# An encoder layer on one core: queries, keys and values of all heads projected in a stage of their own, attention loading finished heads, and GpSimd copying the experts' row numbers

## The reference, cut to what matters

```
q = (rmsnorm(c_q, q_norm_g) @ w_uq).reshape(b, s, N_HEADS, QK_NOPE + QK_ROPE)
kv = (rmsnorm(c_kv, kv_norm_g) @ w_ukv).reshape(b, s, N_HEADS, QK_NOPE + V_DIM)
q = jnp.concatenate([q[..., :QK_NOPE], apply_rope(q[..., QK_NOPE:], cos, sin)], axis=-1)
k = jnp.concatenate([kv[..., :QK_NOPE], jnp.broadcast_to(k_pe, ...)], axis=-1)
...
scores = jnp.einsum('bqhd,bkhd->bhqk', qb, k)
p = jax.nn.softmax(scores, axis=-1)
...
xe = xf[idx]
ye = (silu(xe @ w_gate) * (xe @ w_up)) @ w_down * gates
out = jnp.zeros_like(xf).at[idx].add(ye)
```

## Time and profile before

| | us |
|---|---|
| median of 3 runs | 4414.47 (4413.76 to 4425.7) |
| the profiled execution | 4414.98, span 4413.2 |
| in_proj, without its first loads | about 394 |
| att1, att0 | 1100, 361 |
| experts | 1740 |

### The profile page before, as it was taken

The page is one execution under the profiler, slowest core; times in us unless marked ns, Lnnn a source line. Parts: engine busy times, 40 slices in busy tenths (PEclk is TensorE's granted clock), DMA queues, the critical chain, the costliest instruction groups (busy, mean ns, idle before and its releaser), DMA issues. The chain is left out here.

```text
span 4413.2 us, 56151 instructions
## 1 busy us (share of the span) xinstructions
PE 3867.6 (88%) x19385; PEld 3141.3 (71%) x19385; DVE 2195.6 (50%) x3666; ACT 1947.7 (44%) x3429; POOL 1224.1 (28%) x954
## 2 busy tenths in 40 slices
PE   7799789999999989975999149999999999999992
PEld 1799656766666755653776039999999999999991
DVE  0322167777777756666222764444444444444443
ACT  0444257666667756652322024333343334333432
POOL 0000047767667756652111050000000000000000
PEclk9899889999999989996999559999999999999996
DMA  7221300000000010015443034544444444454436
GB/s 257 99 75 68 99 2 7 4 8 6 8 6 5 6 48 6 13 32 177 153 152 121 2 115 140 155 148 147 143 143 143 151 153 143 145 154 148 143 110 247
DMA packets 296384, 428.21 MB, mean 97 GB/s; under 512 B 43558, under 2 KB 206246, under 8 KB 295050
## 3 DMA queue, kind: packets, MB, share of 16 engines
q1 hardware_dynamic: 269900, 327.41, 22.6%
q0 software_dynamic: 13824, 50.34, 5.1%
q10 hardware_dynamic: 12480, 48.24, 2.8%
HBM read 335.88 MB, written 90.06 MB: 97 GB/s over the span
## 5 line engine op out<-in xcount | busy, mean ns | idle before, releaser
L1114 POOL TENSOR_TENSOR att_pr<-att_e,att_pr 128x512 fp32r<-128x512 f32 x640 | 816.1, 1288 | 399.5 <-ACT att_pr L919 383.6
L982 DVE TENSOR_REDUCE att_mx<-att_m_ps 128x1 f32<-128x512 f32 x640 | 423.0, 680 | 217.6 <-PE att_m_ps L722 214.8
L1954 ACT ACTIVATE moe_wh<-moe_raw 128x1024 fp32r<-128x1024 f32 x384 | 373.9, 1045 | 302.2 <-DMA moe_raw<-w_up 179.5
L913 ACT ACTIVATE att_e<-att_s_ps 128x512 f32<-128x512 f32 x640 | 378.8, 592 | 276.2 <-PE att_s_ps L783 167.6
L1875 POOL DMA_INDIRECT s_x<-moe_ye,moe_to_add x48 | 75.9, 1581 | 1446.0 <-issue 1159.6
L2001 DVE TENSOR_TENSOR moe_wl<-moe_raw,moe_wh 128x1024 fp32r<-128x1024 f32 x384 | 444.5, 1220 | 40.5 <-ACT moe_wh L1954 40.5
L795 PE MATMUL att_o_ps<-att_pr,att_v 128*128 128x512 f32 x1280 | 410.6, 402 | 9.6 <-issue 6.9
L919 ACT ACTIVATE att_pr<-att_e 128x512 fp32r<-128x512 f32 x640 | 402.4, 629 | 16.9 <-issue 1.9
L1911 PE MATMUL moe_a_ps<-moe_xh,moe_wh 128*128 128x384 f32 x1024 | 351.0, 343 | 46.8 <-DVE moe_hf L2029 43.8
L1028 DVE TENSOR_TENSOR att_acc_ps<-att_acc_ps,att_e 128x512 f32<-128x512 f32 x544 | 374.3, 688 | 16.2 <-ACT att_e L913 10.5
L1912 PE MATMUL moe_a_ps<-moe_xl,moe_wh 128*128 128x384 f32 x1024 | 348.7, 341 | 0.0
(11 more groups left out here) (238 smaller groups left out, 7786.0 us busy)
## 6 DMA issues: line engine op xcount, KB each, us to landing
moe_raw<-w_gate SPq DMA_DIRECT2D x64, 1024.0 KB, 5.3
moe_raw<-w_up SPq DMA_DIRECT2D x64, 1024.0 KB, 7.8
moe_raw<-w_down SPq DMA_DIRECT2D x64, 1024.0 KB, 6.7
ada_wa<-w_ada SPq DMA_DIRECT2D x12, 2048.0 KB, 10.0
s_x<-outp_x ACTq DMA_DIRECT2D x24, 512.0 KB, 5.4
s_xn<-outp_xn ACTq DMA_DIRECT2D x24, 512.0 KB, 6.4
fin_x<-s_x SPq DMA_DIRECT2D x12, 1024.0 KB, 12.0
inp_x<-x_sample SPq DMA_DIRECT2D x8, 1024.0 KB, 5.2
```

What stands on the lines that cost most here:

```text
L913: nc.scalar.activation(e[:, s % RING, :], s_ps[s % 2][:, :], ACT.Exp, scale=SCALE).then_inc(exp_done, 1)
L982: nc.vector.tensor_reduce(mx[:, u % CB, u // CB:u // CB + 1], m_ps[u % MB][:, :], AX, ALU.max).then_inc(max_part, 1)
L1114: nc.gpsimd.tensor_tensor(pr[:, s % RING, 1, :], e[:, s % RING, :], pr[:, s % RING, 0, :].bitcast(F32), ALU.subtract).then_inc(lo_done, 1)
L1954: nc.scalar.activation(wh[:, s, part, :], raw[:, s, part, :], ACT.Copy).then_inc(w_hi_done, 1)
```

## The change

`in_proj` stores the latents already split, without the gain: ACT's `latent_high` takes three high parts, DVE three low parts behind the `u_ps` copy, and PE's next turn of latents waits for those (`ct_lo_done`). The rotary key is stored split too, per tile.

A new stage, `latent_proj` (tiles `prj_...`), loads `w_uq` and `w_ukv`, multiplies them by the gain and splits them, and goes over 6 blocks of 512 tokens. Per block PE fills 16 PSUM banks in the order ORDER: four each of keys, queries and values, two of rotary queries (`r`), two of the same with their halves exchanged (`t`). ACT and DVE make high and low parts, and SP stores them to `s_qn`, `s_qr`, `s_kn` and `s_v`.

`attention` no longer projects: SP loads a head's split queries, keys and values into one of HU buffers (2 in att1, 4 in att0) while the head before it is worked on. Its maxima have three PSUM banks (MB = 3) in place of two. In `experts` POOL makes the two copies of row numbers, and DVE waits for `added` only before it writes `ye`.

```diff
@@ in_proj, VectorE, after the copy of u_ps
+                    dve.wait_ge(ct_hi_done, 3 * (n + 1))
+                    hi, lo = (ct[:, n % 2, i, :] for i in range(2))
+                    nc.vector.tensor_tensor(lo[:, 0:BANK], c_ps[0][:, :], hi[:, 0:BANK].bitcast(F32), ALU.subtract)
+                    nc.vector.tensor_tensor(lo[:, BANK:], c_ps[1][:, 0:P], hi[:, BANK:].bitcast(F32), ALU.subtract)
+                    nc.vector.tensor_tensor(krt[:, n % 2, 1, :], c_ps[1][0:ROPE, P:2 * P],
+                                            krt[:, n % 2, 0, :].bitcast(F32), ALU.subtract).then_inc(ct_lo_done, 1)
                     if j == 1 and b + 2 < NB:
                         norm(b + 2)
...
@@ latent_proj, TensorE
+            for b in range(NB):
+                pe.wait_ge(ct_in[b % 2], 16 * (b // 2 + 1))
+                for n, (kind, i) in enumerate(ORDER):
...
+                    ks = KQ if kind in "qrt" else KKV
+                    for k in range(ks):
...
+                        nc.tensor.matmul(dst, a_hi, b_hi, start=(k == 0), stop=False)
+                        nc.tensor.matmul(dst, a_hi, b_lo, start=False, stop=False)
+                        mm = nc.tensor.matmul(dst, a_lo, b_hi, start=False, stop=(k == ks - 1))
+                    mm.then_inc(ready, 1)
...
@@ attention, SyncE
+            def load_qk(n, i):
+                for dst, src in ((q[0:NOPE, i], w["s_qn"]), (q[NOPE:QK, i], w["s_qr"]), (k[0:NOPE, i], w["s_kn"])):
+                    sp.dma_start(dst.bitcast(F32), src[:, bass.ds(n, 1), :, tokens]
+                                 .rearrange("l o r t -> (o r) l t")).then_inc(qk_in[i], 16)
...
@@ attention, TensorE, in body
-                    if kt == KSTEP and project:
...
-                        project_k(x_ps, j, 1 - h)
...
-                    if kt == QPROJ and project:
-                        pe.wait_ge(k_lo_done, hp * NG + NQB + b + 1)
-                        project_q(1 - h, j)
...
@@ experts, GpSimd
+                for s in range(SLOTS):
+                    if not is_first(e):
+                        pool.wait_ge(added[s], e * 16)
+                nc.gpsimd.tensor_copy(to_add[:, :].unsqueeze(1), keep["index"][:, bass.ds(e, 1), :]).then_inc(add_index, 1)
+                pool.wait_ge(ye_done, (e + 1) * DOWNS)
```

More of the change, by code:

```diff
@@ L214, in in_proj @@
         ut = m.sb("ut", [P, 2, UG, T])
-        ct = m.sb("ct", [P, 2, KC * P])
-        krt = m.sb("krt", [ROPE, TOKENS])
-        gain = m.sb("gain", [P, KC])
+        ct = m.sb("ct", [P, 2, 2, KC * P], F32R)
+        krt = m.sb("krt", [ROPE, 2, 2, P], F32R)
         eps = m.sb("eps", [P, 1])
@@ L686, in body @@
+            load_qk(0, 0)
+            for i in range(HU):
+                sp.dma_start(k[NOPE:QK, i].bitcast(F32), w["s_kr"][:, :, tokens]
+                             .rearrange("l r t -> r l t")).then_inc(kpe_in, 16)
+            load_v(0, 0)
+            for i in range(1, HU):
+                load_qk(i, i)
+                load_v(i, i)
+            def body(it, last):
                 for b in range(NG):
                     h, j = b // NQB, b % NQB
-                    if j == 0 and not last:
-                        sp.wait_ge(q_ready, hp * NG + (h + 1) * NQB)
-                        load_weights(hp * 2 + h + 2, h)
@@ L691, in body @@
[L691 to L696 removed]
+                    if j == 0 and from_start(it, h - 1) and not (last and h >= 1):
+                        sp.wait_ge(values_done, it * PER + h * NQB * NT)
+                        load_qk(it * HU + h - 1 + HU, (h - 1) % HU)
+                        load_v(it * HU + h - 1 + HU, (h - 1) % HU)
@@ L697, in _ @@
+                    if from_start(it, b - 1):
+                        store(it, b - 1)
+            over_heads(sp, body)
+            store(ITERS, -1)
             for i in range(2):
-                sp.wait_ge(att_stored[i], 16 * PAIRS * NQB)
+                sp.wait_ge(att_stored[i], 16 * HEADS * NQB // 2)
         @block.tensor
         def _(pe):
-            def project_k(out, j, k0):
-                for k in range(KKV):
-                    mm = nc.tensor.matmul(out[0:NOPE, :], wk[:, k0, k, :], ct_cols(KQ + k, j),
-                                          start=(k == 0), stop=(k == KKV - 1))
-                mm.then_inc(k_ready, 1)
@@ L929, in body @@
+            def body(it, last):
                 for s in range(PER):
                     b, kt, h, j = at(s)
-                    project = not (last and h == 1)
                     if kt == NT - 1 and not (last and b == NG - 1):
-                        act.wait_ge(nmx_turned, hp * NG + b + 2)
+                        act.wait_ge(nmx_turned, it * NG + b + 2)
                         max_row(*after(b))
-                    if from_start(hp, s - 1):
-                        high(hp, s - 1)
-                    exps(hp, s)
@@ L1053, in body, with output @@
+            def output(it, b):
+                dve.wait_ge(osum_done, it * NG + b + 1)
+                dve.wait_ge(rden_spread, it * NG + b + 1)
+                if from_start(it, b - 2):
+                    dve.wait_ge(att_stored[b % 2], 16 * (it * (NG // 2) + b // 2))
+                nc.vector.tensor_tensor(att[:, b % 2, :], osum[:, :], o_ps[b % 2][0:VD, :], ALU.mult).then_inc(att_done, 1)
+            def body(it, last):
                 for s in range(PER):
                     b, kt, h, j = at(s)
-                    project = not (last and h == 1)
@@ L2040, in body @@
                                     x_low(e + 1, k)
+                            if n == 0 and not is_first(e):
+                                dve.wait_ge(added[s], e * 16)
                             dve.wait_ge(d_ready, e * DOWNS + j + 1)
@@ L2142, in build @@
         in_proj(nc, w, keep)
+        latent_proj(nc, w, keep)
         for g in (1, 0):
```

775 lines of the change are left out of this document (370 added, 405 removed).

## The result

The median of the changed kernel is 4243.93 us (4 runs, 4240.71 to 4245.16), against 4414.42 us (4 runs) of the kernel before: ratio 0.9607, 95% interval 0.959 to 0.9624. The forecast was 4262 us with a range of 4220 to 4345. The profiled execution has a span of 4241.9 us in place of 4413.2.

The account below looks back on a forecast made before the run. TensorE was taken to bound the attention blocks, with float32 projection matmuls at four times the F32R price. The terms summed as 4414.98 - 335 + 200 + 44 - 62 = 4262 us, range 4220 to 4345.

Parts of the forecast that it names:

- Part 1: Both attention stages without projections: 335 us less, 244 in att1 and 91 in att0.
- the 12 us of two overlapping halves: att1 setup: loads to lower and upper partitions could overlap on different ports, about 12 us; the forecast stayed with 17.
- the 3 us for a cold clock: att0: 3 us added for a cold clock to fifteen intervals of 14.85 us, making 226.
- the 189 us of the thirty intervals: att1: thirty intervals between rows of maxima fall from 948.8 to 760.2 us, at 25.34 each.
- It matters what it is busy with: Attention: TensorE is busy 93% and 89% of the time; float32 projection matmuls cost four times an F32R one.
- Part 2: New projection stage: adds 200 us, as 21 to fill, 168 of matmuls, 3 cold clock, 8 at the end.
- rival (a): New stage: stores taken one after another last 454 us in place of 173, 4542 us; chance 0.05.
- rival (b): New stage: DMA bounds it mildly at 256 GB/s, 213 us in place of 173, 4302 us; chance 0.14.
- Part 3: in_proj: adds 44 us, 23 from later scaling at ten block ends, 20 from lost clock, 1 at the end.
- Part 4: Experts: row numbers copied on GpSimd end VectorE's wait and TensorE's 43.8 us with it; 62 us less.
- Rival (c): Experts keep their period because TensorE then waits for weights; 4324 us, chance 0.10.
- Rival (e): Attention blocks stay at 27 us, VectorE being the next bound; adds 78 us, 4340 us, chance 0.07.

Follow-up runs that it names:

- either experiment: Changed kernel with the old experts stage put back: 4307.08 us; kernel before with only the new experts stage: 4355.56 us.
- the two fastest kernels: Changed kernel with x scaled before the subtractions and query weights loaded before the first latents: 4199.31 us; that plus first head's high parts loaded first: 4178.45 us.

## Why the prediction was right, step by step

**Part 1, attention, -335: measured -342.1.** The size is right term by term in att1: first row 32.4 us after the load (31.5 forecast, though the terms printed there add up to 31.0), first interval 23.5 (28.3), thirty intervals 763.1 (760.2). Of the 32.4, the load took 20.7 (19), so the 12 us of two overlapping halves did not come; the sixteen maxima took 10.7 (10.5), turn and copy 1.1 (1.5). In att0 the first row came 21.2 us after the load (20), and the fifteen intervals took 218.8 us, not 226: the first two are 13.05 and 12.47 us, and the 3 us for a cold clock were not lost. The reasoning behind the 189 us of the thirty intervals was half blind, though. "It matters what it is busy with" put all of it on the float32 matmuls. By the experiments some 52 us of it (948.8 - 896.3) were TensorE waiting for maxima, and the half clock after that, because the values' split met GpSimd's backlog. They left with the split, which the new stage does. I had the row of 4.60 us in the earlier trace rows and used it only for the clock. The rest of the 185.7 us measured (948.8 - 763.1), 133 us, goes to the matmuls: 28 blocks at 1.93 + 2.73 are 130, of which the runs cut only the queries'. The total came out because I took the interval of the last head, which has neither.

**Part 2, the new stage, +200: measured 195.0.** 12.4 us to the first product, 2.9 us of products, a wait of 9.4 us for split query weights, 163.9 us of unbroken products, 6.4 us to the next stage. I had 21 to fill (12.4 + 9.4 = 21.8). The 166.8 us of products hold two of my terms: at full clock the 720 starts are 0.227 us apart, 163.4 us where I had 168, and behind the two waits fifteen starts at half clock, most of them 0.43 apart, cost the other 3.4, where I had 3. The end took 6.4 us, not 8. One forecast reading was off: the DMA share was to stay under 0.9 and is 0.92. The doubled stores rule out rival (a), and rival (b), DMA at 256 GB/s, too: it sustains 391 to 398. In rival (a) the estimate from 270 us of stores should read 4359 us (4262 + 270 - 173), not 4370. The Trainium skill (DMA: Bandwidth & Descriptors, section Bandwidth) asks for at least 1 MiB a transfer; 512 KB at 391 GB/s show that many in flight do as well here.

**Part 3, in_proj, +44: measured +36.8.** The mechanism is as forecast, and moving the scaling of x back returned 35.3 us. The gap grew by 1.98 us in place of 2.3, 19.8 us over ten, since ScalarE's high parts were there 1.59 us after the start of VectorE's copy and not 2.0; the clock cost the other 17, where I had 20 and 1.

**Part 4, row numbers, -62: measured -61.0** in the profile and 63 by either experiment. Rival (c), that weights take the wait's place, did not happen: from 2620 to 4170 no wait of TensorE above 0.2 us is left.

**Rival (e)**, blocks at 27 us, did not happen: 25.22 to 25.32. The error of 18 us (4262 against 4244) is the sum of four small ones: 7, 5, 7 and -1; three of them lie on the same side.

## What to carry to other kernels

When a unit of work leaves a block, take the new length from a block that never had it, and then ask what else that block lacks: the difference holds waits as well as work, and the waits might have been had for one number. Before code is put between two steps of an engine, find who waits for the second one; ten short stops cost their length twice, once as a wait and once as a lower clock. When a stage gets near two limits at once, cut or double each to see how far the other is.

## What the runs showed of the hardware

- VectorE and GpSimd stop each other over operands. A 128x256 subtraction with both inputs in SBUF takes 0.40 us alone, 1.2 to 1.5 us beside one GpSimd operation, and 3.38 or 5.24 us when GpSimd has a backlog of operations of 1.3 us; with one input in PSUM 0.41 us beside the same backlog. GpSimd is held too: with the pieces moved, its operation that starts at 769.91 beside a piece takes 1.61 us in place of 1.29. In the rows of four a piece that came behind GpSimd's start ended 0.3 us after the last of them, so it had no turn between two. Elsewhere it had one: in the kernel before, a piece from 637.37 to 638.58 ended 0.3 us after one GpSimd operation (637.00 to 638.29), and the next one of GpSimd, from 638.25, took 1.47 us, where it takes 1.30 with one input in PSUM. What decides between the two stays open. The Trainium skill (SBUF — State Buffer, section Who interferes with whom) says that a VectorE instruction with two SBUF inputs contends with a GpSimd instruction that reads SBUF; by that the runs agree, and they add that in the rows of four the wait was as long as what was left of the backlog.
- At one place of att1, where the loop body is entered anew, all engines stop. Timelines of VectorE, TensorE and ScalarE of the kernel after:

```profile
1185.32 0.69 DVE L1057 TENSOR_TENSOR att_acc<-att_acc_ps,att_e 128x512 f32<-128x512 f32 x1 [2.85 <-issue]
1185.42 0.79 PE L923 MATMUL att_s_ps<-att_q,att_k 97*128 97x512 f32 x1 [2.67 <-issue]
1185.58 0.63 ACT L1004 ACTIVATE att_pr<-att_e 128x512 fp32r<-128x512 f32 x1 [2.23 <-issue]
```

  None waits for anything that the profile shows. The kernel before has the stop too, 2.72 us on VectorE. The interval is 30.95 us here, 31.26 with the stores made twice and 27.7 to 28.1 in the six other runs with this attention; the ordinary one is 25.2 to 25.3. The clock makes that difference: over the 8 us behind the stop the granted clock is 0.60 here (0.57 with the stores twice) and 1.00 in the two fastest kernels. What sets the stop itself stays open.
- A copy of 128x3 row numbers is recorded at two lengths on GpSimd. From its timeline in the kernel after, where VectorE took 0.17 us:

```profile
2730.87 1.56 POOL L1863 DMA_INDIRECT s_x<-moe_ye,moe_to_add  x1 [0.30 <-issue]
2731.85 0.77 POOL L1841 COPY moe_to_gather<-keep_index 128x3 int32 x1
2741.15 0.18 POOL L1858 COPY moe_to_add<-keep_index 128x3 int32 x1 [4.08 <-DMA s_x<-moe_ye,moe_to_add]
```

  The copy that starts when GpSimd has nothing else open takes 0.18 us, no more than on VectorE. The one recorded at 0.77 us (14 of 16) starts while GpSimd's own indirect DMA instruction is still open.
